# Identity transposes in TensorE's wait behind a per-layer embedding, and the next block's first product re-ordered by token tile

## The reference, cut to what matters

```
for i in (0, 1):
    x = x + 0.5 * swiglu(rms_norm(x, g[0]), ffn_w_gate[i, 0], ffn_w_up[i, 0], ffn_w_down[i, 0])
    x = x + mixer_i(rms_norm(x, g[1]))            # even mixer, then MLA
    x = x + 0.5 * swiglu(rms_norm(x, g[2]), ...)  # second feed-forward
    x = x + rms_norm(sigmoid(h @ w_gate) * (p_i @ w_proj), g[4])   # PLE, h = rms_norm(x, g[3])
# then a hybrid mixer, a last feed-forward and a last norm
```

## Time and profile before

| | |
|---|---|
| time, median of 3 runs | 1451.99 us (1450.03 to 1452.05) |
| time of the profiled execution | 1452.0 us |
| its span, first to last instruction | 1450.1 us |
| mean granted TensorE clock | 0.96 |
| busy: TensorE, VectorE, ScalarE | 95%, 56%, 45% |

### The profile page before, as it was taken

The page is one execution under the profiler, slowest core; times in us unless marked ns, Lnnn a source line. Parts: engine busy times, 40 slices in busy tenths (PEclk is TensorE's granted clock), DMA queues, the critical chain, the costliest instruction groups (busy, mean ns, idle before and its releaser), DMA issues.

```text
span 1450.1 us, 17440 instructions
## 1 busy us (share of the span) xinstructions
PE 1370.9 (95%) x6616; PEld 1133.1 (78%) x6616; DVE 805.3 (56%) x837; ACT 652.4 (45%) x734; POOL 88.9 (6%) x176
## 2 busy tenths in 40 slices
PE   6999997998999998999999899999997999999996
PEld 5888886776888887788887767888886987788885
DVE  4554568645555455545456655554555885554543
ACT  5434354523543445543435634534345653544342
POOL 2000013300000001000000200000001200000000
PEclk9999998989999999899999979999999996999998
DMA  7555553333555555355554304655553450366560
GB/s 254 191 186 188 188 171 106 116 117 117 196 196 180 190 187 174 116 187 190 190 186 146 116 29 137 204 174 193 183 198 122 146 191 29 128 206 196 180 200 32
DMA packets 158699, 233.29 MB, mean 161 GB/s; under 512 B 7496, under 2 KB 124894, under 8 KB 158654
## 3 DMA queue, kind: packets, MB, share of 16 engines
q1 hardware_dynamic: 156004, 229.19, 47.3%
q10 hardware_dynamic: 2170, 2.68, 0.6%
q0 software_dynamic: 480, 0.80, 0.2%
HBM read 231.58 MB, written 1.05 MB: 160 GB/s over the span
## 4 chain that ended last, share of the span: by engine, by line
PE 85%; DVE 8%; ACT 4%; issue 1%; POOL 1%; DMA 1%; SPq 0%; POOLq 0%; ACTq 0%; DVEq 0%
PE ps L231 25%; PE ps L233 25%; PE ps L232 24%; PE ps L1200 2%; DVE wl L203 2%; PE ps L500 2%; ACT wh L198 2%; PE ps L312 1%; PE ps L906 1%; DVE x_rows L442 1%; PE ps L247 1%; PE ps L249 1%; PE ps L248 1%; DMA raw<-in_ffn_w_up 1%; DVE htl L345 1%
## 5 line engine op out<-in xcount | busy, mean ns | idle before, releaser
L231 PE MATMUL ps<-wl,hth 128*128 128x512 f32 (+2 forms) x1274 | 507.5, 398 | 29.2 <-DVE wl L203 13.0
L233 PE MATMUL ps<-wh,htl 128*128 128x512 f32 (+2 forms) x1274 | 499.2, 392 | 0.0
L232 PE MATMUL ps<-wh,hth 128*128 128x512 f32 (+2 forms) x1274 | 499.1, 392 | 0.0
L663 DVE TENSOR_TENSOR wl<-raw,wh 128x2048 fp32r<-128x2048 f32 x120 | 275.1, 2292 | 204.8 <-ACT wh L612 204.8
L231 PEld LDWEIGHTS ps<-wl,hth 128*128 128x128 f32 x1274 | 243.7, 191 | 80.6 <-issue 16.4
L203 DVE TENSOR_TENSOR wl<-raw,wh 128x2048 fp32r<-128x2048 f32 (+2 forms) x99 | 222.2, 2256 | 132.1 <-ACT wh L198 132.0
L612 ACT ACTIVATE wh<-raw 128x2048 fp32r<-128x2048 f32 x120 | 229.6, 1914 | 123.7 <-PE ps L233 123.7
L233 PEld LDWEIGHTS ps<-wh,htl 128*128 128x128 f32 x1274 | 243.2, 191 | 51.3
L232 PEld LDWEIGHTS ps<-wh,hth 128*128 128x128 f32 x1274 | 244.3, 192 | 47.8
L198 ACT ACTIVATE wh<-raw 128x2048 fp32r<-128x2048 f32 (+2 forms) x99 | 184.3, 1872 | 87.2 <-PE ps L233 66.0
L231 PE MATMUL ps<-wl,prod_h 128*128 128x512 f32 x400 | 156.1, 390 | 0.0
(11 more groups left out here) (313 smaller groups left out, 1012.8 us busy)
## 6 DMA issues: line engine op xcount, KB each, us to landing
raw<-in_ffn_w_gate SPq DMA_DIRECT2D x88, 512.0 KB, 4.0
raw<-in_ffn_w_up SPq DMA_DIRECT2D x88, 512.0 KB, 5.0
raw<-in_ffn_w_down SPq DMA_DIRECT2D x88, 512.0 KB, 3.9
raw<-in_w_gate_up SPq DMA_DIRECT2D x44, 512.0 KB, 4.7
raw<-in_even_w_in SPq DMA_DIRECT2D x24, 512.0 KB, 4.6
raw<-in_w_down SPq DMA_DIRECT2D x22, 512.0 KB, 4.1
raw<-in_ple_w_gate SPq DMA_DIRECT2D x16, 512.0 KB, 3.8
raw<-in_w_in SPq DMA_DIRECT2D x16, 512.0 KB, 4.5
```

Source lines behind the costliest of these rows:

```text
L231: nc.tensor.matmul(o, xh, b, start=first, stop=False)
L232: nc.tensor.matmul(o, xh, a, start=False, stop=False)
L233: return nc.tensor.matmul(o, xl, a, start=False, stop=last)
L663: nc.vector.tensor_tensor(wl[:, r, :], raw[:, r, :], wh[:, r, :].bitcast(f32), ALU.subtract)\
```

## The change

Three edits. TensorE, when it has done a PLE's products and tile 0's sigmoid has been made, transposes the identity (128 x 128) into PSUM bank 4, 24 times in the first PLE and 48 times in the second; nothing reads the result, and the bank is written again or started anew before it is next read. In the first PLE alone, VectorE adds tile 0's update to x (`add(0)`) ahead of tile 1's gating (`gated(1)`). In the feed-forward behind it, TensorE's transposes of tile 1 stand inside tile 0's product, behind its feature block k = 5, and no longer after the whole of it.

```diff
             def first_by_tiles(pe):
 
+                turn_tile(pe, s, 0, 0)
+                turn_tile(pe, s, 0, 1)
                 for tt in range(TT):
-                    turn_tile(pe, s, tt, 0)
-                    turn_tile(pe, s, tt, 1)
                     for u in range(2):
                         take_slot(pe, n + u)
                         turned_by(pe, s, 0, 2 * tt + u + 1)
@@
                             m = product(bank(tt), hth[:, k, tt * P:(tt + 1) * P], htl[:, k, tt * P:(tt + 1) * P],
                                         wh[:, r, at:at + 2 * HC], wl[:, r, at:at + 2 * HC], k == 0, k == KT - 1)
+                            if tt == 0 and k == 5:
+                                turn_tile(pe, s, 1, 0)
+                                turn_tile(pe, s, 1, 1)
                         if tt == TT - 1:
                             m.then_inc(weights_used, 1)
@@ ple_pe, at its end
+            pe.wait_ge(ple_gate.sem, ple_gate.after("sigmoid0", l))
+            for _ in range(24 if after_ple(s + 1) else 48):
+                nc.tensor.transpose(ps[:, 4, 0:P], ident[:, :], ident[:, :])
@@ ple_dve
             gated(0)
             gain(0)
-            gated(1)
-            add(0)
+            if after_ple(s + 1):
+                add(0)
+                gated(1)
+            else:
+                gated(1)
+                add(0)
             if after_ple(s + 1):
                 tile_dve(dve, s + 1, 0, 0, FFN_GAIN[fs[s + 1]])
             gain(1)
```

## The result

| | before | changed |
|---|---|---|
| first comparison, median (range, executions) | 1452.02 us (1450.03 to 1452.13, 4) | 1441.68 us (1440.7 to 1442.6, 4) |
| profiled execution: time, span, mean clock | 1452.0, 1450.1 us, 0.960 | 1442.6, 1440.1 us, 0.973 |

The ratio is 0.9932, 95% interval 0.9915 to 0.9949: 10 us faster, where I had forecast 2.1 us and a range down to 1447.6. The prediction was wrong. A second comparison with more executions (experiment 5) has 1441.3 us against 1448.6 us in the mean, 7.3 us, and a reported ratio of 0.9961 (0.9940 to 0.9982), which is 5.6 us (2.6 to 8.7).

The account below looks back on a forecast made before the run. TensorE, busy for 95% of the span, was taken as the bound, through idle time and half clock. Terms 1.15 + 0 - 1.36 - 1.67 - 0.2 = -2.1 us gave 1449.9 us; range of 8 in 10: 1447.6 to 1452.6 us.

Parts of the forecast that it names:

- +1.15 us forecast for tile 0's product: First PLE: add(0) ahead of gating 1 delays squares 1 on ScalarE, so tile 0's product starts 1.15 us later.
- the 1.36 us: Feed-forward behind the first PLE: turning tile 1 ahead of six of tile 0's matmuls saves 1.36 us.
- the 1.67 us: Tile 1's product: idle time ahead shrinks to 0.8 us, so its half-clock loss of 1.67 us goes.
- tile 0's half clock: Tile 0's product behind the first PLE: same half-clock loss as before, 2.12 us, so 0 us change.
- The slack of the third slot: Behind tile 1's product: slack of the third slot's low half shrinks from 2.24 to 0.6 us, without a stall.
- the 2.5 us of idle time: Behind the second PLE: the 48 transposes shrink TensorE's idle stretch from 7.80 to 2.5 us.
- part 3: Tile 1 turned inside tile 0's product: -1.36 and -1.67 us; a 0.47 us matmul behind 1.50 us idle meant clock up.
- Rival A: The clock never falls behind the first PLE: 2.12 us more gained, 1447.2 us in all; chance 0.13.
- rival B: Transposes don't hold the clock, so tile 1's 1.67 us and the second PLE's 0.2 us stay lost: 1451.8 us; chance 0.12.
- part 4: Second PLE's 48 identity transposes: less idle time, clock holding one time in four, -0.2 us.
- The -0.2 us for the second PLE: Saving on the 16 transposes of x if the clock holds there: -0.2 us, bounds 0 and -1.3.
- the sum's basis: Whole kernel: 1452.0 us profiled, executions moving by 2 us, changes within 0.2% (2.9 us) hardly measurable.

Follow-up runs that it names:

- experiment 5: The changed kernel, unedited, run again in 12 executions beside the kernel before: mean 1441.3 us, reported ratio 0.9961.
- Experiment 8: Changed kernel without the reorder, with 38 and 68 identity transposes and 18 more ahead of tile 0's product: mean 1439.2 us, ratio 0.9946.
- experiment 4: Changed kernel without the reorder, add(0) back behind gating 1: mean 1442.0 us, ratio 0.9949.
- experiments 3: Kernel before plus only the 48 identity transposes behind the second PLE: mean 1445.9 us, ratio 0.9976.
- experiments 1: Kernel before plus only the identity transposes, 24 and 48, no other edit: mean 1445.5 us, ratio 0.9981.
- 2: Changed kernel without any identity transposes, keeping the reorder and the turning inside the product: mean 1447.4 us, ratio 0.9981.
- 7: Kernel before plus only tile 1's turning inside tile 0's product: mean 1445.8 us, ratio 0.9978.

## Why the prediction was wrong

**Right**: the order of releases behind the first PLE. The reorder makes x earlier and its use later (+1.15 us forecast for tile 0's product, +1.02 measured: 8.82 us behind the last product in place of 7.80), ScalarE's squares 1 being what holds the tile up. The turning inside the product: 3.09 us kept, the 1.36 us and the 1.67 us gained. Together with tile 0's half clock, which cost 1.47 us where I had put the 2.12 of before, the place gave -2.56 us; I had -1.88. The slack of the third slot sufficed: no stall behind tile 1. Behind the second PLE the 2.5 us of idle time was right (2.56). One sign in part 3 was read too easily: a first matmul of 0.47 us does not show that the clock stays up, since the one at 592.12 took 0.47 us too and its stretch had a mean clock of 0.76. Rival A's sum comes to 1447.35 us, not 1447.2.

**The rule on transposes** (the Trainium skill, TensorE: Matmul & The Clock Gate, Part 4: PE-mode transpose): in the changed kernel TensorE does nothing but 64 transposes from 1112.2 to 1122.2, with 2.56 us of idle time between, and the clock is 1.00 over the whole fourth stretch. Experiment 8 has 1.00 over 20.62 us in which 38 and 18 of them filled the idle time, where experiment 4, with 24 and idle time left, had 22.21 us. The page says that transposes don't count as busy for the clock in the way matmuls do. Here they hold it, against the page, and rival B falls. They don't do so over every gap: experiments 3 and 4 have the same 48 transposes and the same 2.56 us of idle time, and the clock fell.

**The step that failed** is in part 4 and the sentence behind the sum: "Both places are followed by TensorE at work without a break, so what is gained there is kept." What was gained is kept; but TensorE is not at work without a break behind it, as the prediction's own rows show: 2.52 us idle ahead of 796.67 and 2.40 us ahead of 1251.68. And I treated the stages behind as passing a shift on unchanged. They don't. In the attention TensorE is busy with short matmuls, and when the clock falls there depends on the moment at which they come. The attention takes 28.08 us when it is at half clock from 1.9 us on (mean 0.53) and 20.7 us when it is at full clock for the first 16.4 us or more (mean 0.90), so a shift decides over 5 to 7 us, about twice what the edits bring directly. The term was missing from the sum; it measured -5.27 us in the first pair of profiles and -4.88 in the second (25.61 to 20.73). The sixth stretch added -2.11 us in the first pair and nothing in the second (216.46 to 216.53), the third -1.10 and -0.95.

The -0.2 us for the second PLE was mis-sized too, and its bound of -1.3 was too narrow: -0.45 us in one pair of profiles, -1.98 in the other (81.39 to 79.41). I had read the bound from one execution, in which the half clock ended with the turning, at about 1125; in the second profile of the kernel before it lasted to about 1128, into the products.

**The second failure** is the sum's basis: "the kernel itself moves by 2 us between executions". I read three executions as the kernel's spread. It is 19 us, in two groups 7 us apart, and the 2.9 us beyond which I called a difference measurable are less than half of that distance. The first 10 us were in part luck of the draw, the four executions of the kernel before having times of its slower group; with more executions it is 7.3 us by the means and 5.6 by the reported ratio.

Why the changed kernel meets the good moment reliably (in its profiles twice, and in 9 of its 12 executions in experiment 5 the mean clock is 0.972 or more, against 3 of the 90 of before) is not shown. The profiles of experiments 1 and 8 and both of the changed kernel (the first and experiment 5) have the clock up all the way from the second PLE to the attention, 79.41 us each, and then 20.73 or 20.74 us. Where it fell behind the second PLE (before twice, 2, 3, 4, 7), that way took 79.86 to 81.39 us and the attention 25.5 to 26.0 us in five of six, 21.50 in the sixth. So the transposes may act by making this distance a fixed one. That is not shown: experiments 3 and 4 had the 48 as well and 80.02 and 80.06 us. That the moment of the second PLE itself then comes right, from one execution to the next, was seen and not explained. Nor was it tried whether the kernel before gets the attention's gain by a delay alone, which is the rival left open.

## What to carry to other kernels

When a sum of local terms is small, look for stages behind it that have two speeds: here short matmuls that ran at half clock or not, with the same instructions. A shift of 1 us ahead of such a stage made the attention alone 7.35 us longer (20.73 to 28.08); list these stages with both prices, and put them into the range. Compare means over many executions sorted by the mean clock before believing a difference of under 1%, and don't take three for the spread. When an update is put ahead of other work on one engine, follow the engine that consumes it: if that one has the displaced work's successor first in its queue, the update comes early and is used late.

## What was not expected of the hardware

- A delay of 1.0, 2.0 and 3.4 us gave 28.08, 25.63 and 20.73 us for the same matmuls, with 20.73 us at no delay: the moment counts, and not monotonically. (The traces list 106 or 107; a record can be missing.)
- In the attention the clock stays where it is for long: before the change it was at 0.50 for most of it with TensorE busy for 23.78 of 26.00 us; so being busy with short matmuls did not bring it back. The clock fell in all thirteen attentions.
- An idle stretch of 2.56 us behind 48 transposes held the clock in some profiles and not in others (B of 79.41 and 80.02 us). Nor is it the kernel that decides: the 2.40 us ahead of the last feed-forward ended in a first matmul of 0.77 us in one profile of the kernel before and of 0.47 us in the other.
